# Reordering VectorE's weight splits among the turns of a dilated attention, with one early exponential on ScalarE

## The chip, the cores and the metric

The kernel runs on one core of a Trainium2 chip. The metric is the device time in microseconds (us) of one execution; lower is better. The engines of the core work in parallel, each through its own list of instructions in order, and meet only at semaphores: TensorE (PE, with its weight loads as PEld), VectorE (DVE), ScalarE (ACT), GpSimd (POOL) and SyncE (SP), which issues the transfers.

## The reference

Four layers of a transformer on 256 tokens of width 1024: two layers of a first kind (feed-forward, mixer, feed-forward), whose mixers differ, and two of a second kind. All is float32. The change lies in the mixer of the second layer, the "odd" one:

```python
def odd_mixer(h, w_in, w_out, q_g, k_g, pool_w, pool_scale):
    q, k, v, u = jnp.split(h @ w_in, [hd, 2 * hd, 3 * hd], axis=-1)
    q = rms_norm(q.reshape(b, s, DIL_HEADS, HEAD_DIM), q_g)      # 8 heads of 64
    k = rms_norm(k.reshape(b, s, DIL_HEADS, HEAD_DIM), k_g)
    outs, ms, ls = zip(*[dilated_branch(q, k, v, w, d) for w, d in DIL_PAIRS])
    ms = jnp.stack(ms)
    wts = jnp.stack(ls) * jnp.exp(ms - jnp.max(ms, axis=0))
    att = jnp.einsum('rbsh,rbshd->bshd', wts, jnp.stack(outs).astype(jnp.float32))
    att = (att / jnp.sum(wts, axis=0)[..., None]).astype(h.dtype)
    pool = multiscale_pool(u, pool_w, pool_scale)
    return jnp.concatenate([att.reshape(b, s, hd), pool], axis=-1) @ w_out
```

The three dilated branches are folded into one attention: scores plus a mask, an exponential, and a multiplication of the exponentials by a table that holds how many branches see each key. Then `x = x + mix`, and a feed-forward block on `rms_norm(x)` follows.

## The kernel before

**Weights.** All weights of the kernel go through one plan of units, mostly 128 x 1024 floats. SP brings unit u into one of six `staging` buffers; ACT makes its high part `whi` (line 1222); DVE subtracts to get the low part `wlo` (line 1710). Both parts live in rings of four buffers, so ACT may make `whi` of unit u only when PE has used unit u - 4. PE multiplies each pair of high and low parts three times (lines 591 to 593) in the mixers, or by the lines 640 and 642 in the feed-forward blocks. The pair "ACT split, DVE split" of one unit is called a split below. Each engine's program counts the splits that it owes in `side.due`, and `catch_up()` writes them out.

**The order.** Nothing is scheduled by a planner. Each engine's list is written by generators that `weave` runs in rounds: in each round every live generator writes its piece up to its next `yield`, and after the round, if a generator is still alive, `after` (here `catch_up`) writes the splits that are due.

**The odd stage, from 698 to 763 us of the trace.** The generator `dil` writes the attention, `pool` the pooled branch and then `down`, the multiplication by `w_out` (eight units, each in two halves of six matmuls). `attend` goes through eight groups of two heads (four for the first 128 tokens, four for the last 128) in turns. For a group i, in successive turns: PE makes the scores (line 833, "scores i"); DVE adds the mask and takes the maximum (line 1982, two instructions and 1991); ACT makes the exponential (line 1370); DVE multiplies by the table and sums (line 1968); PE transposes the result (line 820); ACT copies it out of PSUM (line 1361); PE multiplies it with v (line 807). After the fourth and the eighth group DVE takes the reciprocal of the sums (line 1945) and writes the attention's output of this half (line 1960, `od_o`). Groups are numbered 0 to 7.

**PSUM.** There are eight banks, handed out by the order of PE's program; who takes a bank waits until its last user's content was read. While `down` holds four of them, the scores of group i + 1 take the bank pair of the scores of group i, so PE's line 833 waits for DVE's line 1982 of the group before. The output of the second half (groups 4 to 7) takes the bank of the first half, so PE's line 807 of group 4 waits for DVE's line 1960 of the first half.

**The end of the stage.** DVE adds `down`'s result to x (line 1758, four instructions). `norm_T` then belongs to the next feed-forward block: PE transposes x in eight pieces (line 603), ACT writes the high part of each piece (`hT`, line 1235), DVE the low part (`hT`, line 1719), after which both write the splits still due. In the feed-forward block PE's first matmul (line 640) waits for the low parts of the pieces 0 and 1: its two banks held these pieces.

Of the kernel before, what the change touches and what calls it, by code (L numbers as in the profile page):

```python
# [10 lines left out]
ALU = mybir.AluOpType  # L11
ACT = mybir.ActivationFunctionType
# [176 lines left out]
def weave(gens, after=None):  # L189

    live, r = list(gens), 0
    while live:
        r += 1
        for item in list(live):
            if r >= item[0]:
                try:
                    next(item[1])
                except StopIteration:
                    live.remove(item)
        if live and after is not None:  # L200
            after()


def build(nc, A, out):
    ctx = ExitStack()
    with ctx:
        K = Count(nc, ctx)
# [1001 lines left out]
        def scalar_program(e):  # L1209
# [231 lines left out]
            def odd(m):  # L1441
                g = m.g
                norm_T(m)

                def project(q):
                    yield from x_cols(512)
                    by_token(g, 512 * q, 512, lambda t: m.qkv[:, t, q * 512:(q + 1) * 512])

                def norm(P, q):
                    sl = slice(512 * q, 512 * q + 512)  # L1450
                    head_norm(P, m.qkv[:, :, sl], m.hq[:, :, sl], [("in ev", g, 512 * q, t) for t in range(2)])

                weave([(1, project(1))], catch_up)
                norm("od k", 1)
                weave([(1, project(0))], catch_up)

                def pool():
                    for j0 in (0, 2):
                        yield
                        split()  # L1460
                        side.due += 1
                        yield
                    for k in range(3):
                        side.due += 1
                        yield
                    yield
                    by_token(g, 1024, 512, lambda t: m.qkv[:, t, 1024:1536])
                    side.due += 1

                def finish():  # L1470
                    for k in range(4):
                        e.wait_ge(*K.at("od pool mm", k))
                        e.activation(m.mh[:, 4 + k, :], bk("od pool", k)[:, 0:256], ACT.Copy,
                                     scale=m.psc[:, k:k + 1]).then_inc(*K.inc("pool_hi", ("od mh", k)))
                    yield
                    yield from down(m.rows)

                def dil():
                    norm("od q", 0)
                    yield  # L1480
                    e.wait_ge(*K.at("par", g))
                    heads_T("od k", 128, 4, m.kT, m.qg[:, 1:2])
                    heads_T("od q", 128, 4, m.qT, m.qg[:, 0:1])
                    yield
                    yield
                    turns = attend(m.at)
                    for _ in range(4):
                        next(turns)
                        yield
                    yield  # L1490
                    yield
                    yield from turns
                    transposed("dil", 4, m.mh[:, 0:4, :])

                weave([(1, dil()), (1, pool()), (9, finish())], catch_up)
# [203 lines left out]
        def vector_program(e):  # L1699
# [63 lines left out]
            def down(g, rows, coef):  # L1763
                for k in range(len(rows)):
                    for n in range(2):
                        if k + 1 == len(rows):
                            for t in range(2):
                                residual(g, coef, t, n)
                        if n and k + 2 < len(rows):
                            side.due += 1  # L1770
                        if n == 0 or k + 1 < len(rows):
                            yield
                side.due += 2
# [133 lines left out]
            def transposed(P, nk, dh, dl, *last):  # L1907
                for k0 in range(0, nk, 2):
                    e.wait_ge(*K.at(P + " oT hi", k0))
                    e.tensor_tensor(flat(dl[:, k0:k0 + 2, :]), bk(P + " oT", k0)[:, 0:512],  # L1910
                                    flat(dh[:, k0:k0 + 2, :]).bitcast(F32), ALU.subtract).then_inc(
                        *K.inc("oTl", (P + " oT", k0 // 2), ("ev", (P + " oT", k0)),
                               *(last if k0 + 2 == nk else ())))
# [9 lines left out]

                return e.tensor_tensor(x, x, r.unsqueeze(2).broadcast_to([128, H, 64]), ALU.mult)

            def attend(a):
                P, H = a.P, a.H
                groups = [(t, h0) for t in range(2) for h0 in range(0, H, 2)]
                mx = a.mx
                scale = a.scale if callable(a.scale) else lambda t, h: a.scale  # L1930
                for turn in range(H + 3):
                    if 0 <= turn - 2 < H and groups[turn - 2][1] == H - 2:

                        i = turn - 2
                        t, c0 = groups[i][0], groups[i][0] * 8
                        l, r = mx[:, 2, c0:c0 + H], mx[:, 3, c0:c0 + H]
                        if a.mult is None:
                            e.wait_ge(*K.at(P + " ex", i))
                        else:
                            e.wait_ge(*K.at(P + " pm", i))  # L1940
                        if a.sink is not None:
                            e.wait_ge(*K.at(P + " sink", t))
                            e.tensor_tensor(l, l, r, ALU.add).then_inc(*K.inc("att_sum"))
                            e.wait_ge(*K.now("att_sum"))
                        e.reciprocal(r, l).then_inc(*K.inc("att_sum", (P + " one by", t)))
                    if 0 <= turn - 3 < H:
                        t, h0 = groups[turn - 3]
                        if h0 == H - 2:
                            r = mx[:, 3, t * 8:t * 8 + H]
                            e.wait_ge(*K.at(P + " one by", t))  # L1950
                            e.wait_ge(*K.at(P + " pv", turn - 3))
                            if a.crossed:
                                o = a.dst[:, t, :].rearrange("p (j i e) -> p i j e", j=2, i=4)
                                src = bk(P + " o", t)[:, 0:512].rearrange("p (i j e) -> p i j e", i=4, j=2)
                                rr = r.rearrange("p (i j) -> p i j", i=4).unsqueeze(3).broadcast_to([128, 4, 2, 64])
                            else:
                                o = a.dst[:, t, :].rearrange("p (h e) -> p h e", h=H)
                                src = bk(P + " o", t)[:, 0:H * 64].rearrange("p (h e) -> p h e", h=H)
                                rr = r.unsqueeze(2).broadcast_to([128, H, 64])
                            e.tensor_tensor(o, src, rr, ALU.mult).then_inc(  # L1960
                                *K.inc("att_sum", (P + " o", t), ("ev", (P + " o", t))))
                    if 0 <= turn - 1 < H and a.mult is not None:
                        i = turn - 1
                        t, h0 = groups[i]
                        nk, c0 = 128 * (t + 1), t * 8 + h0
                        e.wait_ge(*K.at(P + " ex", i))
                        for j in range(2):
                            e.tensor_tensor_reduce(out=a.sm[i % 3][:, j, 0:nk], in0=a.sm[i % 3][:, j, 0:nk],
                                                   in1=a.mult(t), scale=1.0, scalar=0.0, op0=ALU.mult, op1=ALU.add,
                                                   accum_out=mx[:, 2, c0 + j:c0 + j + 1]).then_inc(  # L1970
                                *K.inc("att_pm", *([(P + " pm", i)] if j else [])))
                    if turn < H:
                        i = turn
                        t, h0 = groups[i]
# [141 lines left out]
            def odd(m):  # L2116
# [17 lines left out]
                def pool():  # L2134
# [44 lines left out]
                    side.due += 1  # L2179
                    yield  # L2180
                    yield from down(g, m.rows, 1.0)

                def dil():
                    head_norm("od q", m.hq[:, :, 0:512], m.hr[0][:, :, :], 8, 64, 64.0)
                    yield
                    yield
                    yield
                    e.wait_ge(*K.at("consts", 1))
                    e.wait_ge(*K.at("od q", "hn"))
                    turns = attend(m.at)  # L2190
                    for _ in range(4):
                        next(turns)
                        yield
                    yield
                    yield
                    yield from turns
                    transposed("dil", 4, m.mh[:, 0:4, :], m.ml[:, 0:4, :])

                weave([(1, dil()), (1, pool())], catch_up)

            def mixer2(m):
                g, P, N = m.g, m.P, m.N
# [506 lines left out]
```

## Time and profile before

| | |
|---|---|
| three runs | 1801.32, 1804.37, 1805.64 us; median 1804.37 |
| the profiled execution | 1804.61 us, of which the span of the trace 1802.8 |
| PE busy | 1778.0 us, 99% of the span |
| DVE busy | 1272.8 us, 71% |
| ACT busy | 947.8 us, 53% |
| 16 transfer engines, main queue | 56.4% of their time |
| granted TensorE clock, mean | 0.998 of full speed |

PE is busy all the time, and 90% of the chain of work that ended last lies on it. In the odd stage the chain leaves PE several times for ACT and DVE. A time in the rows is in us from the span's start.

### The profile page before, as it was taken

Reading aid. Unit: us, or ns where it says so; the run is one execution under the profiler, and the core shown is the slowest. Engines: PE = TensorE matmul, PEld = TensorE weight load, DVE = VectorE, ACT = ScalarE, POOL = GpSimd, SP = SyncE. Lnnn points to the kernel's source line nnn. Section 1 sums busy time; section 2 is a strip of 40 time slices with the busy share of each in tenths; the row PEclk is TensorE's granted clock in tenths of the full one; section 3 lists DMA queues with packets and bytes.
Section 4 is the critical chain, followed back from the end, with each engine's and each line's share of the span. In section 5 each row is a group of like instructions: output and inputs, shape, how many; then the busy total and the mean of one; then the engine's idle time right before and its main releaser. Section 6 shows DMA issues by size and latency. Waiting matters only on the chain.

```text
span 1802.8 us, 24902 instructions
## 1 busy us (share of the span) xinstructions
PE 1778.0 (99%) x9704; PEld 1512.2 (84%) x9704; DVE 1272.8 (71%) x1932; ACT 947.8 (53%) x1344; POOL 30.1 (2%) x38
## 2 busy tenths in 40 slices
PE   8999999999999999999999999999999999999998
PEld 7888888888888888788888788888888878888886
DVE  6775795776577657677656967777756778677774
ACT  5554655555455545565535545455544644555553
POOL 0000000000000001000000000000000000000000
PEclk9999999999999999999999999999999999999999
DMA  8666523666566655366666534556665443456663
GB/s 252 197 179 199 174 83 92 197 184 194 167 203 186 194 174 181 106 188 189 196 186 179 171 113 130 183 181 188 193 191 172 141 154 123 157 185 191 190 194 106
DMA packets 227614, 309.25 MB, mean 172 GB/s; under 512 B 22494, under 2 KB 176254, under 8 KB 227498
## 3 DMA queue, kind: packets, MB, share of 16 engines
q1 hardware_dynamic: 227334, 307.35, 56.4%
q8 instruction: 78, 1.28, 0.3%
q14 instruction: 38, 0.31, 0.1%
q10 hardware_dynamic: 164, 0.30, 0.1%
HBM read 306.57 MB, written 1.05 MB: 171 GB/s over the span
## 4 chain that ended last, share of the span: by engine, by line
PE 90%; DVE 6%; ACT 2%; issue 1%; DMA 1%; SPq 0%; DVEq 0%; POOLq 0%; POOL 0%; ACTq 0%
PE ps L640 26%; PE ps L591 15%; PE ps L593 15%; PE ps L592 15%; PE ps L642 13%; DVE wlo L1710 2%; PE ps L1132 1%; PE ps L603 1%; PE ps L807 1%; DVE ev_acc L1719 1%; PE ps L833 1%; ACT whi L1222 1%; PE ps L820 1%; PE ps L775 0%; DVE m_scr L1719 0%
## 5 line engine op out<-in xcount | busy, mean ns | idle before, releaser
L1710 DVE TENSOR_TENSOR wlo<-staging,whi 128x1024 fp32r<-128x1024 f32 (+1 forms) x582 | 695.0, 1211 | 344.9 <-ACT whi L1222 344.6
L1222 ACT ACTIVATE whi<-staging 128x1024 fp32r<-128x1024 f32 (+1 forms) x582 | 608.1, 1050 | 484.8 <-PE ps L593 297.9
L640 PE MATMUL ps<-hT,whi 128*128 128x512 f32 x1984 | 624.5, 396 | 0.0
L642 PEld LDWEIGHTS ps<-hT,wlo 128*128 128x128 f32 x1984 | 373.0, 188 | 88.2
L642 PE MATMUL ps<-hT,wlo 128*128 128x256 f32 x1984 | 390.0, 278 | 0.0
L640 PEld LDWEIGHTS ps<-hT,whi 128*128 128x128 f32 x1984 | 302.4, 189 | 0.2 <-DVE hT L1719 0.2
L591 PE MATMUL ps<-whi,fh 128*128 128x512 f32 (+1 forms) x528 | 206.0, 390 | 0.4 <-DVE wlo L1710 0.4
L592 PE MATMUL ps<-wlo,fh 128*128 128x512 f32 (+1 forms) x528 | 205.5, 389 | 0.0
L593 PE MATMUL ps<-whi,fl 128*128 128x512 f32 (+1 forms) x528 | 205.3, 389 | 0.0
L591 PE MATMUL ps<-whi,hT 128*128 128x512 f32 (+3 forms) x464 | 184.7, 398 | 0.8 <-DVE wlo L1710 0.6
L593 PE MATMUL ps<-whi,hT 128*128 128x512 f32 (+3 forms) x464 | 177.4, 382 | 0.0
L592 PE MATMUL ps<-wlo,hT 128*128 128x512 f32 (+3 forms) x464 | 177.0, 381 | 0.0
L591 PEld LDWEIGHTS ps<-whi,fh 128*128 128x128 f32 (+1 forms) x528 | 99.1, 188 | 22.6 <-DVE wlo L1710 2.3
L593 PEld LDWEIGHTS ps<-whi,fl 128*128 128x128 f32 (+1 forms) x528 | 99.1, 188 | 20.7
L592 PEld LDWEIGHTS ps<-wlo,fh 128*128 128x128 f32 (+1 forms) x528 | 99.1, 188 | 20.3
L591 PEld LDWEIGHTS ps<-whi,hT 128*128 128x128 f32 x464 | 87.2, 188 | 21.4 <-issue 3.8
L593 PEld LDWEIGHTS ps<-whi,hT 128*128 128x128 f32 x464 | 87.2, 188 | 16.2
L592 PEld LDWEIGHTS ps<-wlo,hT 128*128 128x128 f32 x464 | 87.4, 188 | 14.3 <-issue 0.5
L1293 ACT ACTIVATE fh<-sg 128x512 fp32r<-128x512 f32 x62 | 39.2, 632 | 114.0 <-DVE sg L1812 114.0
L1797 DVE TENSOR_TENSOR sg<-sg,R 128x512 f32<-128x512 f32 x124 | 85.8, 692 | 4.3
L1794 DVE TENSOR_TENSOR sg<-ps,sg 128x512 f32<-128x512 f32 x124 | 84.9, 684 | 0.2
L591 PE MATMUL ps<-hT,whi 128*128 128x256 f32 x288 | 82.8, 287 | 0.0
(328 smaller groups left out, 1870.2 us busy)
## 6 DMA issues: line engine op xcount, KB each, us to landing
staging<-in_w_in SPq DMA_DIRECT2D x92, 512.0 KB, 3.6
staging<-in_ffn_w_down SPq DMA_DIRECT2D x88, 512.0 KB, 4.2
staging<-in_ffn_w_gate SPq DMA_DIRECT2D x84, 512.0 KB, 4.3
staging<-in_ffn_w_up SPq DMA_DIRECT2D x84, 512.0 KB, 4.5
staging<-in_w_ffn_gate SPq DMA_DIRECT2D x44, 512.0 KB, 4.5
staging<-in_w_ffn_up SPq DMA_DIRECT2D x44, 512.0 KB, 4.5
staging<-in_w_ffn_down SPq DMA_DIRECT2D x44, 512.0 KB, 4.2
staging<-in_od_w_in SPq DMA_DIRECT2D x16, 512.0 KB, 4.4
```

The source lines that it names most:

```text
L591: e.matmul(o, lh, rh, start=start, stop=False)
L592: e.matmul(o, lh, rl, start=False, stop=False)
L593: return e.matmul(o, ll, rh, start=False, stop=stop)
L603: w = e.transpose(ps[:, t * 128:t * 128 + 128], xs[:, t, k * 128:k * 128 + 128], ident)
L640: e.matmul(o, wh[:, kk, j * 128:j * 128 + 128], hT[:, k, :], start=k == 0, stop=False)
L642: m = e.matmul(o[:, 0:256], wl[:, kk, j * 128:j * 128 + 128], hTh[:, k, :], start=False, stop=k == KD - 1)
L807: w = e.matmul(ops[t][:, (h0 + j) * 64:(h0 + j) * 64 + 64], a.pt[i % 2][:, o:o + 128], a.vN(kt, h0 + j), start=kt == 0, stop=kt == t)
L1222: e.activation(whi[u % NH][:, 0:n], stage[u % NS][:, 0:n], ACT.Copy).then_inc(*K.inc("hi", ("hi", u)))
L1293: e.activation(f.fh[:, 2 * p:2 * p + 2, :], s[:, :, 0:256], ACT.Copy).then_inc(*K.inc("fh", ("fh", g, p, 0)))
L1710: e.tensor_tensor(wlo[u % NH][:, 0:n], stage[u % NS][:, 0:n], whi[u % NH][:, 0:n].bitcast(F32), ALU.subtract).then_inc(*K.inc("lo", ("lo", ...
L1794: e.tensor_tensor(ss, PS[:, b:b + 2, 0:256], ss, ALU.add).then_inc(*K.inc("ps_r", *[("ev", u) for u in users]))
L1797: e.tensor_tensor(ss, ss, R22, ALU.mult).then_inc(*K.inc("ps_r", ("scaled", g, p, part)))
```

## The change

In the odd stage, three things. On DVE, `attend` gets a parameter `between`, and the multiplication by the table (line 1968 before) moves ahead of the block of line 1960; between the two `between()` writes the splits that are due. For the odd stage `between` is `catch_up`, and `dil` also calls `catch_up` in its rounds without a turn. `weave` gets no `after` any more there. At the end `dil` goes on until `pool` has finished (`over`), and a last `catch_up()` follows the `weave`. On ACT, one exponential of one column is written two rounds ahead of the turns, its result in a column that nothing reads. The other attentions have no table and no `between`; their order stays.

```diff
+                    e.activation(m.at.mx[:, 3, 8:9], m.qg[:, 0:1], ACT.Exp).then_inc(*K.inc("exp"))
                     yield
                     turns = attend(m.at)
...
-            def attend(a):
+            def attend(a, between=lambda: None):
...
+                    if 0 <= turn - 1 < H and a.mult is not None:
+                        ...
+                                *K.inc("att_pm", *([(P + " pm", i)] if j else [])))
+                    between()
                     if 0 <= turn - 3 < H:
...
                     yield from down(g, m.rows, 1.0)
+                    over.append(True)
+
+                over = []
...
                     yield
-                    yield
-                    yield
+                    for _ in range(2):
+                        catch_up()
+                        yield
...
-                    turns = attend(m.at)
+                    turns = attend(m.at, catch_up)
...
                     yield from turns
                     transposed("dil", 4, m.mh[:, 0:4, :], m.ml[:, 0:4, :])
-
-                weave([(1, dil()), (1, pool())], catch_up)
+                    while True:
+                        yield
+                        catch_up()
+                        if over:
+                            return
+
+
+                weave([(1, dil()), (1, pool())])
+                catch_up()
```

What this does to the lists of the engines, at three places. Names in the rows: `od_0` to `od_2` are the exponentials of three groups in turn, `od_3` and `od_4` their transposes, `od_5` maxima and sums. In the changed kernel the line numbers are higher: 1710 is 1712, 1968 is 1955, 1960 is 1974, 1982 is 1986, 1719 is 1721. An ISA row on two heads is the multiplication or the masked maximum of one head.

First place: DVE, from the scores of group 5 to the scores of group 6. Before:

```order
L1991 TENSOR_SCALAR od_5<-od_5 128x2 [waits s_att_mx]
L1710 TENSOR_TENSOR wlo0<-staging,whi0 128x1024 [waits s_hi]
L1960 TENSOR_TENSOR od_o<-ps,od_5 128x512 [waits s_att,s_att_sum]
L1968 ISA od_2,od_5<-od_2,cst 128x256 [waits s_exp]
L1968 ISA od_5 128x1
L1982 ISA od_0,od_5<-ps,cst,od_hr0 128x256 [waits s_att]
```

In the changed kernel:

```order
L1995 TENSOR_SCALAR od_5<-od_5 128x2 [waits s_att_mx]
L1955 ISA od_2,od_5<-od_2,cst 128x256 [waits s_exp]
L1955 ISA od_5 128x1
L1712 TENSOR_TENSOR wlo0<-staging,whi0 128x1024 [waits s_hi]
L1974 TENSOR_TENSOR od_o<-ps,od_5 128x512 [waits s_att,s_att_sum]
L1986 ISA od_0,od_5<-ps,cst,od_hr0 128x256 [waits s_att]
```

The split and the output of the first half stood ahead of the multiplication of group 5 and now stand behind it. (Each multiplication and each masked maximum has a second pair of rows for the second head.)

Second place: DVE, the end of the odd stage. Before:

```order
L1710 TENSOR_TENSOR wlo1<-staging,whi1 128x1024 [waits s_hi]
L1758 TENSOR_TENSOR xs<-ps,xs 128x512 [waits s_prod] x4
L1719 SCALAR_TENSOR_TENSOR hT<-ps,gcol,hT 128x256 [waits s_hTh] x8
L1710 TENSOR_TENSOR wlo2<-staging,whi2 128x1024 [waits s_hi]
L1710 TENSOR_TENSOR wlo3<-staging,whi3 128x1024 [waits s_hi]
```

In the changed kernel:

```order
L1712 TENSOR_TENSOR wlo1<-staging,whi1 128x1024 [waits s_hi]
L1760 TENSOR_TENSOR xs<-ps,xs 128x512 [waits s_prod] x4
L1712 TENSOR_TENSOR wlo2<-staging,whi2 128x1024 [waits s_hi]
L1712 TENSOR_TENSOR wlo3<-staging,whi3 128x1024 [waits s_hi]
L1721 SCALAR_TENSOR_TENSOR hT<-ps,gcol,hT 128x256 [waits s_hTh] x8
```

Two splits moved from behind the eight low parts to ahead of them. On ACT the same place is unchanged:

```order
L1222 ACTIVATE whi2<-staging 128x1024
L1235 ACTIVATE hT<-ps,gcol 128x256 x8
L1222 ACTIVATE whi3<-staging 128x1024
```

ACT writes `whi2` ahead of its eight high parts and `whi3` behind them, in both kernels.

Third place: ACT, ahead of the first turn. Before:

```order
L1337 ACTIVATE od_qT<-ps,od_qg 128x512 x2
L1222 ACTIVATE whi0<-staging 128x1024
L1222 ACTIVATE whi1<-staging 128x1024
L1222 ACTIVATE whi2<-staging 128x1024
L1222 ACTIVATE whi3<-staging 128x1024
L1370 ACT_TABLE_LOAD
L1370 ACTIVATE od_0<-od_0,od_5 128x128 x2
```

In the changed kernel:

```order
L1337 ACTIVATE od_qT<-ps,od_qg 128x512 x2
L1222 ACTIVATE whi0<-staging 128x1024
L1222 ACTIVATE whi1<-staging 128x1024
L1486 ACT_TABLE_LOAD
L1486 ACTIVATE od_5<-od_qg 128x1
L1222 ACTIVATE whi2<-staging 128x1024
L1222 ACTIVATE whi3<-staging 128x1024
L1370 ACTIVATE od_0<-od_0,od_5 128x128 x2
```

The load of the exponential's table moved ahead of two splits, with the one-column exponential behind it.

## Rows read from the trace of the kernel before

**Rows 1.** The page, part 1: busy us (share of the span), instructions.
```profile
PE 1778.0 (99%) x9704; PEld 1512.2 (84%) x9704; DVE 1272.8 (71%) x1932; ACT 947.8 (53%) x1344; POOL 30.1 (2%) x38
```

**Rows 2.** Waits, 700 to 765 us: us in total, times, longest us.
```profile
PE ps L820 <- DVE od L1968: 1.6, 3, 0.9
...
PE ps L787 <- DVE od_o L1960: 0.9, 1, 0.9
```

**Rows 3.** ACT in order of time: start us, us, instruction [idle before <- releaser].
```profile
707.67 1.06 ACT L1222 ACTIVATE whi<-staging 128x1024 fp32r<-128x1024 f32 x1 [3.85 <-PE ps L593]
709.11 1.06 ACT L1222 ACTIVATE whi<-staging 128x1024 fp32r<-128x1024 f32 x1 [0.37 <-PE ps L593]
710.19 1.28 ACT L1370 ACT_TABLE_LOAD   x1
711.48 0.70 ACT L1370 ACTIVATE od<-od 128x128 f32<-128x128 f32 x2
```

**Rows 4.** PE in order of time, three places of the turns.
```profile
723.91 1.89 PE L951 MATMUL ps<-od_pl,od_pw 128*128 128x256 f32 x8
...
729.90 0.70 PE L833 MATMUL ps<-od_kT,od_qT 64*128 64x256 f32 x4 [0.21 <-DVE od L1982]
...
735.26 1.10 PE L807 MATMUL ps<-od_qkv,od 128*128 128x64 f32 x8
```

**Rows 5.** DVE in order of time, end of the pooling and groups 3 and 4.
```profile
723.05 0.22 DVE L2170 TENSOR_TENSOR od_pl<-od_pl,od_u 128x64 f32<-128x64 f32 x1
...
727.30 1.23 DVE L1710 TENSOR_TENSOR wlo<-staging,whi 128x1024 fp32r<-128x1024 f32 x1 [0.43 <-ACT whi L1222]
728.44 0.28 DVE L1968 CUSTOM_DVE_ANT_0 od<-od,cst 128x128 f32<-128x128 f32 x1
...
728.86 0.48 DVE L1982 CUSTOM_DVE_ANT_0 od<-ps,cst,od_hr 128x256 f32<-128x256 f32 x1
```

**Rows 6.** ACT in order of time, the exponentials of groups 3 and 5.
```profile
727.43 0.69 ACT L1370 ACTIVATE od<-od 128x128 f32<-128x128 f32 x2
...
733.73 0.90 ACT L1370 ACTIVATE od<-od 128x256 f32<-128x256 f32 x2
```

**Rows 7.** DVE in order of time, groups 5 and 6.
```profile
734.52 0.68 DVE L1960 TENSOR_TENSOR od_o<-ps,od 128x512 f32<-128x512 f32 x1
735.12 0.42 DVE L1968 CUSTOM_DVE_ANT_0 od<-od,cst 128x256 f32<-128x256 f32 x1
...
735.81 0.48 DVE L1982 CUSTOM_DVE_ANT_0 od<-ps,cst,od_hr 128x256 f32<-128x256 f32 x1
```

**Rows 8.** DVE in order of time, the end of the stage.
```profile
759.34 2.74 DVE L1758 TENSOR_TENSOR xs<-ps,xs 128x512 f32<-128x512 f32 x4 [1.02 <-PE ps L593]
762.11 3.22 DVE L1719 SCALAR_TENSOR_TENSOR hT<-ps,gcol,hT 128x256 fp32r<-128x256 f32 x8
```

**Rows 9.** ACT in order of time, the same stretch.
```profile
758.71 1.06 ACT L1222 ACTIVATE whi<-staging 128x1024 fp32r<-128x1024 f32 x1 [1.66 <-PE ps L593]
761.60 3.03 ACT L1235 ACTIVATE hT<-ps,gcol 128x256 fp32r<-128x256 f32 x8 [1.82 <-PE ps L603]
764.47 1.11 ACT L1222 ACTIVATE whi<-staging 128x1024 fp32r<-128x1024 f32 x1
```

**Rows 10.** PE in order of time, the same stretch.
```profile
761.18 2.10 PE L603 MATMUL ps<-cst,xs 128*128 128x128 f32 x16
763.08 0.70 PE L640 MATMUL ps<-hT,whi 128*128 128x512 f32 x2
```

**Rows 11.** Stretches of the even stage: PE, PEld, DVE, ACT, POOL busy; PEclk, transfers.
```profile
277.80:281.07 3.27, 2.70 (x25) 2.73 (x26) 1.71 (x3) 2.93 (x4) 0.00 (x0) 1.00 0.00 0
281.07:284.48 3.41, 3.41 (x10) 2.64 (x10) 0.64 (x3) 0.35 (x1) 0.70 (x1) 0.50 0.00 0
```

**Rows 12.** PE in order of time, the same stage.
```profile
278.37 1.06 PE L787 MATMUL ps<-cst,ev_o 128*128 128x128 f32 x8 [1.17 <-DVE ev_o L1960]
...
279.27 1.84 PE L914 MATMUL ps<-cst,ev_sqc 128*128 128x1 f32 x16
```

More of the change, by code:

```diff
@@ L1945, in attend @@
                         e.reciprocal(r, l).then_inc(*K.inc("att_sum", (P + " one by", t)))
+                    if 0 <= turn - 1 < H and a.mult is not None:
+                        i = turn - 1
+                        t, h0 = groups[i]
+                        nk, c0 = 128 * (t + 1), t * 8 + h0
+                        e.wait_ge(*K.at(P + " ex", i))
+                        for j in range(2):
+                            e.tensor_tensor_reduce(out=a.sm[i % 3][:, j, 0:nk], in0=a.sm[i % 3][:, j, 0:nk],
+                                                   in1=a.mult(t), scale=1.0, scalar=0.0, op0=ALU.mult, op1=ALU.add,
+                                                   accum_out=mx[:, 2, c0 + j:c0 + j + 1]).then_inc(
+                                *K.inc("att_pm", *([(P + " pm", i)] if j else [])))
+                    between()
                     if 0 <= turn - 3 < H:
@@ L1961, in attend @@
                                 *K.inc("att_sum", (P + " o", t), ("ev", (P + " o", t))))
[L1962 to L1971, printed above, removed]
                     if turn < H:
@@ L2193, in dil @@
                         yield
-                    yield
-                    yield
+                    for _ in range(2):
+                        catch_up()
+                        yield
                     yield from turns
                     transposed("dil", 4, m.mh[:, 0:4, :], m.ml[:, 0:4, :])
-                weave([(1, dil()), (1, pool())], catch_up)
+                    while True:
+                        yield
+                        catch_up()
+                        if over:
+                            return
+                weave([(1, dil()), (1, pool())])
+                catch_up()
             def mixer2(m):
```

## The prediction

> **What bounds the kernel now.** I read the page's busy times first: PE is busy 99% of the span [rows 1]. Whatever holds PE up is paid in full, and what happens on DVE, ACT or the transfer queues counts only where PE waits for it. The waits of the odd stage come next: PE stands 1.6 us before its transposes (line 820) for DVE's multiplication by the table, and once 0.9 us (line 787) for the attention's output [rows 2]. That is about 2.5 us, and it is all that a better order of the turns can give back. Then I read the three engines side by side, in order of time, wherever the new lists differ: in the turns, and at the end of the stage. The end of the stage is the place that a reader of the diff misses.
>
> **The change part by part.**
>
> *The early exponential.* Before, ACT finishes a split at 710.17, loads the table for 1.28 us and starts the first exponential at 711.48 [rows 3]. Now the load lies ahead of the split that starts at 707.67, where ACT stood idle for 3.85 us waiting for PE [rows 3]. Load and one short exponential, under 2 us together, vanish in that idle stretch, so they cost nothing; were it absent they would cost 1.28 us and a bit. The first exponential starts 1.28 us earlier, the first multiplication follows, and the first transposes, one of the waits in [rows 2], are no longer late: some 0.6 us for PE.
>
> *The splits behind the multiplication, turns 1 to 3.* A split holds DVE 1.14 us from start to start (727.30 to 728.44) [rows 5]. Taken out from ahead of the second multiplication, it lets that one run 1.14 us earlier, and PE's longest wait of 0.9 us [rows 2] goes. PE is then about 1.3 us ahead. But it next needs the pooled tensor, which ends 723.05 + 0.22 = 723.27 on DVE, while PE starts on it at 723.91 [rows 5, 4]: a margin of 0.64. DVE has no idle time there to give up, since it does the same work in another order; I find it 0.1 us earlier at most. So PE is about 0.7 us ahead at the pooling matmuls.
>
> *Group 3 and 4.* Before, DVE waits for ACT's high part, does the split at 727.30, and meets the exponential of group 3 (ended 728.12) at 728.44; the scores of group 4 start at 728.86 [rows 5, 6]. Now the exponential ends at 728.12 - 0.67 = 727.45. Multiplication 0.42, then the split 1.14, then the scores: 729.05 in place of 728.86. The split, which filled DVE's wait for the exponential, now stands between the multiplication and the scores. PE's scores of group 5 wait for the scores of group 4 to be read, since they share the banks; they started at 729.90 [rows 4], now at about 730.1. The lead of 0.7 us is gone and PE is 0.2 us behind.
>
> *Group 5 and 6.* The same thing, larger. The exponential of group 5 runs 733.73 to 734.63 [rows 6]; 0.2 later it ends at 734.8. Before, DVE did a split and the half's output (line 1960, started 734.52, over at 735.20) during that exponential, multiplied at 735.12 and began the scores of group 6 at 735.81 [rows 7]. Now it idles until 734.8, multiplies for 0.69 (735.12 to 735.81), splits for 1.14 and only then writes the output: 736.64, over at 737.32. PE's line 807 of group 4 takes the bank of that output. It began at 735.26, right behind the output [rows 4, 7]; now it begins at about 737.4. Price: 2.1 us, less at most 0.1 of a wait that stood there anyway. This shift carries through groups 6 and 7, for each of the following steps hangs on the one before (scores, exponential, multiplication, transposes), and the last split before the second output waits for PE's own progress. **The turns together: 2.0 us lost.** The bounds: 2.5 us gained, if the waits of [rows 2] go and nothing takes their place; 4 us lost, if a second split is exposed besides.
>
> *The end of the stage.* Before, DVE starts the low parts of the transposed x at 762.11, right after x [rows 8], and PE's first matmul of the feed-forward block starts at 763.08, as soon as the pieces 0 and 1 are there (762.11 + 2 x 0.40 + 0.05 = 762.96; 3.22 us for eight) [rows 8, 10]. Now two splits come first. The first finds its high part (ACT, 758.71) ready and takes 762.11 to 763.25. The second needs the high part that ACT writes behind its own eight high parts: it starts at 764.47 and ends at 765.58 [rows 9]. So DVE waits until 765.61, splits until 766.75, and then starts the low parts: pieces 0 and 1 are there at 767.6, and PE starts at 767.7 in place of 763.08. **4.6 us lost**, in which PE has nothing at all to do, since its transposes end at about 763.2 [rows 10]. Behind it PE needs 0.7 us per piece and DVE delivers one each 0.4 [rows 8, 10], so nothing more is lost; and nothing comes back, since the two splits were never late (they are the third and fourth unit of the block, wanted 5 us after its start). Bounds: 4 us, if ACT's split follows a little faster, and 5, by the durations of [rows 8, 9].
>
> *TensorE's clock.* After such a pause the clock is likely to fall. In the even stage, after a stretch in which PE idled 1.17 us before line 787 and then did sixteen matmuls of one column [rows 12], the granted clock was 0.50, the level of 1.2 GHz, for 3.41 us (281.07 to 284.48), against 1.00 (2.4 GHz) before [rows 11]. At half speed 3.41 us do the work of 1.7. The new pause is 4.6 us with nothing in it, longer than the thin stretch above. Price: **1.7 us**, between 0 and 3.4 (two such stretches). By the Trainium skill ("TensorE: Matmul & The Clock Gate", sections "What's actually happening" and "HAM oscillation"), an idle PE falls back to half clock, and the first matmuls behind a wait run cold; the trace's 0.50 behind a thin stretch agrees, and by that page the sum would hold the 1.7 us, by the mean clock of 0.998 alone it would not.
>
> *Transfers.* Splits set free the staging buffers. Five are 0.1 to 2 us later, two are earlier; the ring is six units deep and no PE wait in the stage names a transfer [rows 2]. Nothing.
>
> **The sum.** The profiled execution took 1804.61 us with a span of 1802.8, and the median of three runs is 1804.37; the rest around the span stays. 1804.6 + 2.0 + 4.6 + 1.7 = 1812.9 us.
>
> **The rivals.** *The clock stays up.* For it: PE was fully busy until 763, and it dropped only once in the span. Against it: the pause is the longest in the trace after the start. Time: 1804.6 + 6.6 = 1811.2. *The turns gain.* If the output of the first half isn't what holds PE at 735.26, the turns save about 1 us: 1804.6 - 1.0 + 4.6 + 1.7 = 1809.9. For it: the waits of [rows 2] are real and the split leaves their path. Against it: the output ends at 735.20 and PE starts at 735.26 [rows 4, 7], and the bank is the same. *The clock falls in the turns too*, at the 2.1 us pause before line 807: another 1.7, so 1814.6. *The other side: the end of the stage costs nothing.* This would be so if PE's transposes and bank waits, and not DVE's low parts, set the start at 763.08, and if DVE's second split found its high part ready. It decides at ACT's split of 764.47: done by 763.2, the low parts would be late by two splits, 2.3 us; only with both splits already done would it be nothing. With the turns gaining all of 2.5 us the time is 1802.1. Against it: ACT's list puts that split behind eight instructions of 3.03 us [rows 9]. *Only the turns cost*, the end being hidden: 1806.6.
>
> **How the numbers follow.** About 0.3% (5.4 us) is what a measurement of this kernel can tell from no change. Forecast with the clock falling once 0.50 (1812.9); clock stays 0.17 (1811.2); turns gain 0.15 (1809.9); clock falls twice 0.08 (1814.6); other side 0.05 (1802.1); only the turns 0.05 (1806.6). The line for slower is 1809.8. The first two and the fourth lie beyond it; the third sits on it and is split; of the rest a little is lost to scatter: slower 0.80, same 0.18, faster 0.02. The range leaves out the last two and the tails: 1808.0 to 1815.5.
>
> **What the new profile would show.** ACT's table load near 704 us, in idle time. PE's transposes of the first two groups without a wait. A wait of PE at line 807 of about 2 us for the output (line 1974), near 735 us. A wait of PE of about 4.5 us, or a gap of that length, between line 603 and line 640 at 765 us, with DVE's two splits ahead of its eight low parts and the second one waiting for ACT. A stretch with PEclk 0.50 behind it. The feed-forward blocks and the layers of the second kind of the same length as before. I am wrong if the stretch from line 603 to the first line 640 keeps its 1.9 us, or if the stage up to line 603 is shorter than before.

## The result, and the profile after

| | before | changed |
|---|---|---|
| median | 1804.37 us (1801.32 to 1805.92, 5 runs) | 1816.3 us (1811.78 to 1817.62, 5 runs) |
| ratio, changed to before | | 1.0059, 95% interval 1.0045 to 1.0073 |
| profiled execution | 1804.61 us, span 1802.8 | 1817.15 us, span 1815.4 |
| granted TensorE clock, mean | 0.998 | 0.994 |

The changed kernel is slower by 0.6%, which the ratio makes 10.6 us (8.1 to 13.2). The page's busy times of the changed kernel answer to [rows 1]:

```profile
PE 1783.8 (98%) x9704; PEld 1516.4 (84%) x9704; DVE 1273.0 (70%) x1932; ACT 948.3 (52%) x1345; POOL 30.1 (2%) x38
```

DVE and ACT do the same work in the same busy time. PE's busy time grew by 5.8 us though its instructions are the same, and the span by 12.6: PE worked slower for part of the time, and stood still for the rest. Where it stood still is in the waits of the changed kernel from 698 to 790 us (us in total, times, longest us), which answer to [rows 2]:

```profile
PE ps L640 <- DVE hT L1721: 4.4, 1, 4.4
...
PE ps L807 <- DVE od_o L1974: 2.0, 1, 2.0
...
PE ps L833 <- DVE od L1986: 1.1, 1, 1.1
...
PE ps L787 <- DVE od_o L1974: 0.9, 1, 0.9
```

PE's waits at line 820, at which the change was aimed, fell from 1.6 us to 0.3, and the 0.9 us at line 787 is as before. New are the waits at the lines 640, 807 and 833. In order of time on PE; the whole program of this trace runs 1.20 us behind the trace of before when the turns begin (line 775 at 699.09 against 697.89), so 1.20 is to be taken off to compare with [rows 4]:

```profile
717.35 0.41 PE L820 MATMUL ps<-cst,od 128*128 128x128 f32 x2 [0.18 <-DVE od L1955]
724.23 1.99 PE L951 MATMUL ps<-od_pl,od_pw 128*128 128x256 f32 x8 [0.35 <-DVE od_pl L2174]
731.17 0.70 PE L833 MATMUL ps<-od_kT,od_qT 64*128 64x256 f32 x4 [1.05 <-DVE od L1986]
738.50 1.10 PE L807 MATMUL ps<-od_qkv,od 128*128 128x64 f32 x8 [1.98 <-DVE od_o L1974]
```

The pooling matmuls start at 723.03 on the time axis of before, 0.88 us ahead of 723.91; the scores of group 5 at 729.97, level with 729.90; line 807 of group 4 at 737.30, 2.04 us behind 735.26. DVE's side of the last one, which answers to [rows 7]: it idles for the exponential, multiplies, splits, and writes the output last.

```profile
735.93 0.43 DVE L1955 CUSTOM_DVE_ANT_0 od<-od,cst 128x256 f32<-128x256 f32 x1 [1.93 <-ACT od L1370]
...
736.63 1.22 DVE L1712 TENSOR_TENSOR wlo<-staging,whi 128x1024 fp32r<-128x1024 f32 x1
737.76 0.68 DVE L1974 TENSOR_TENSOR od_o<-ps,od 128x512 f32<-128x512 f32 x1
```

The end of the stage, DVE, then ACT, then PE, for [rows 8 to 10]:

```profile
762.49 2.74 DVE L1760 TENSOR_TENSOR xs<-ps,xs 128x512 f32<-128x512 f32 x4 [1.02 <-PE ps L593]
765.14 1.22 DVE L1712 TENSOR_TENSOR wlo<-staging,whi 128x1024 fp32r<-128x1024 f32 x1
768.76 1.23 DVE L1712 TENSOR_TENSOR wlo<-staging,whi 128x1024 fp32r<-128x1024 f32 x1 [2.40 <-ACT whi L1222]
769.90 3.22 DVE L1721 SCALAR_TENSOR_TENSOR hT<-ps,gcol,hT 128x256 fp32r<-128x256 f32 x8
```

```profile
764.75 3.03 ACT L1235 ACTIVATE hT<-ps,gcol 128x256 fp32r<-128x256 f32 x8 [1.82 <-PE ps L603]
767.62 1.11 ACT L1222 ACTIVATE whi<-staging 128x1024 fp32r<-128x1024 f32 x1
```

```profile
764.33 2.10 PE L603 MATMUL ps<-cst,xs 128*128 128x128 f32 x16
770.87 0.81 PE L640 MATMUL ps<-hT,whi 128*128 128x512 f32 x2 [4.44 <-DVE hT L1721]
771.91 1.05 PE L640 MATMUL ps<-hT,whi 128*128 128x512 f32 x2
```

From line 603 to line 640 PE takes 6.54 us, where it took 1.90. The last row shows more: two matmuls of 512 columns span 1.05 us, against 0.70 in [rows 10]. The clock fell. Stretches of the changed kernel (PE, PEld, DVE, ACT, POOL busy; PEclk, transfers):

```profile
270.00:300.00 30.00, 27.87 (x137) 23.39 (x136) 14.04 (x26) 14.90 (x26) 0.70 (x1) 0.89 0.13 36
698.00:748.00 50.00, 46.28 (x290) 38.23 (x288) 34.57 (x108) 28.06 (x48) 2.90 (x1) 1.00 0.37 111
764.00:790.00 26.00, 21.56 (x121) 18.58 (x120) 15.24 (x25) 14.31 (x23) 0.70 (x1) 0.93 0.36 98
1000.00:1200.00 200.00, 197.88 (x1078) 161.93 (x1078) 152.04 (x296) 98.49 (x158) 3.40 (x3) 0.99 0.48 148
1400.00:1600.00 200.00, 197.63 (x1094) 163.03 (x1094) 149.49 (x305) 99.71 (x159) 3.40 (x3) 0.99 0.48 147
```

PEclk is below 1.00 after the pause, but also in the even stage (0.89; the same stretch of before has 0.94) and in the mixers of the two layers of the second kind (0.99 over 200 us is one stretch at 1.2 GHz, 3.4 us long), where no instruction was changed. What PE did ahead of the first of these two stretches, which begins at 1051.20:

```profile
1048.85 1.50 PE L1132 MATMUL ps<-m_scr 32*128 32x128 f32 x16 [0.88 <-DVE m_scr L1986]
```

**Three lengths** make all that follows comparable, since they do not hold what happened elsewhere in the execution. *Turns*: from the start of the first transposes of keys and queries (line 775) to the start of the transposes of x (line 603). *Pause*: from there to the first line 640; 2.1 us of it are the transposes, so PE's own wait is shorter (4.44 us of the 6.54). *Block*: from there to the transposes at the end of the feed-forward block (line 603, 943.89 before, 953.22 after). Before they are 63.29, 1.90 and 180.81 us; in the changed kernel 65.24, 6.54 and 182.35. The differences are 1.95, 4.64 and 1.54, together 8.13 us. The other 4.5 us of the difference of the spans lie outside: 1.2 ahead of line 775, and 3.2 in the two mixers, 1.6 for each stretch at 1.2 GHz. The experiments ask what causes the 8.1, and whether the 4.5 belong to the change. The profiled execution, at 1817.15 us, is one of the slower ones of the five.

### The profile page after: what moved, and what is told of

It reads as the page before. It is cut to its first block, busy times and chain, and to the rows that moved or that the text cites. A ratio compares the mean times of both kernels' runs of the same rounds, so it can differ in the third digit from the quotient of the medians.

```text
span 1815.4 us, 24903 instructions
## 1 busy us (share of the span) xinstructions
PE 1783.8 (98%) x9704; PEld 1516.4 (84%) x9704; DVE 1273.0 (70%) x1932; ACT 948.3 (52%) x1345; POOL 30.1 (2%) x38
## 3 DMA queue, kind: packets, MB, share of 16 engines
HBM read 306.57 MB, written 1.05 MB: 169 GB/s over the span
## 4 chain that ended last, share of the span: by engine, by line
PE 89%; DVE 6%; ACT 2%; issue 1%; DMA 1%; SPq 0%; DVEq 0%; POOLq 0%; POOL 0%; ACTq 0%
PE ps L640 26%; PE ps L591 15%; PE ps L592 14%; PE ps L593 14%; PE ps L642 13%; DVE wlo L1712 2%; PE ps L1132 1%; PE ps L807 1%; PE ps L603 1%; DVE ev_acc L1721 1%; ACT whi L1222 1%; PE ps L833 1%; PE ps L820 1%; PE ps L775 0%; DVE m_scr L1721 0%
```

## The experiments

All times are medians of each kernel's runs and of the kernel before on the same chip; the ratio is of the two, with its 95% interval. The lengths are those of one trace each.

**The end of the stage alone.** In the kernel before:

```diff
                 weave([(1, dil()), (1, pool())], catch_up)
+                catch_up()
```

> The kernel before, with one line more on VectorE: the two splits that are due at the end of the odd stage are written ahead of the low parts of the transposed x, as in the changed kernel. Theory (the end of the stage costs 4.6 us, the clock 1.7): the turns keep their length (63.3 us from line 775 to line 603), the stretch from the transposes (line 603) to the first matmul of the feed-forward block (line 640) grows from 1.9 to 6.5 us, a stretch of 1.2 GHz follows, and the time is about 6.3 us above before. Rival (the delay at the end is a follow-up of the slower turns): the stretch stays near 1.9 us and the time near before.

1811.13 us against 1804.66, ratio 1.0035 (1.0023 to 1.0048). Turns 63.30, pause 6.54, block 183.09. On PE:

```profile
763.97 2.10 PE L603 MATMUL ps<-cst,xs 128*128 128x128 f32 x16
770.51 1.19 PE L640 MATMUL ps<-hT,whi 128*128 128x512 f32 x2 [4.44 <-DVE hT L1719]
```

One line at the end makes the whole pause, to the hundredth of a microsecond, with unchanged turns. The clock fell already within the pause and stayed down behind it (PEclk by stretch):

```profile
768.20:770.50 2.30, 0.00 (x0) 0.02 (x1) 2.10 (x4) 2.21 (x5) 0.00 (x0) 0.61 0.42 147
770.50:775.10 4.60, 4.59 (x14) 3.93 (x15) 2.34 (x7) 0.14 (x2) 0.70 (x1) 0.50 0.41 118
```

So this block lost 2.3 us to the clock, not 1.5. 4.64 + 2.28 = 6.9 us for this trace; the ratio of the medians makes 6.3 (4.2 to 8.7 by the interval). The theory holds, the rival is out.

**The turns alone.** In the changed kernel, the last `catch_up()` taken out, and the end of `dil` turned round so that nothing is written once `pool` has finished:

```diff
                     while True:
                         yield
-                        catch_up()
                         if over:
                             return
+                        catch_up()
...
                 weave([(1, dil()), (1, pool())])
-                catch_up()
```

> The changed kernel with the end of the stage as before: the two splits behind the low parts again. Theory: the stretch from line 603 to line 640 is back at 1.9 us, the turns stay 2.0 us longer (65.2 us from line 775 to line 603), and the time is about 2 us above before. Rival (the clock alone makes the excess over the pauses, also in other stages): the time stays more than 4 us above before.

1808.45 us against 1804.66, ratio 1.0019 (1.0008 to 1.0029), that is 3.4 us (1.4 to 5.2). Pause 1.90, block 180.80: the end is repaired. Whether the time is about 2 us above before or over 4, the interval does not say; the lengths decide. The turns took 66.79 us, not 65.2. The clock tells why:

```profile
734.00:737.40 3.40, 2.43 (x14) 2.10 (x16) 1.89 (x7) 0.37 (x1) 0.00 (x0) 0.77 0.54 149
737.40:741.00 3.60, 3.60 (x19) 2.59 (x18) 1.76 (x9) 1.65 (x4) 0.00 (x0) 0.74 0.01 5
```

Behind the wait of 2 us at line 807 the clock was down, which it was not in the changed kernel's first trace. That asked for more traces, below.

**The early exponential alone.** In the kernel before:

```diff
                     heads_T("od q", 128, 4, m.qT, m.qg[:, 0:1])
                     yield
+                    e.activation(m.at.mx[:, 3, 8:9], m.qg[:, 0:1], ACT.Exp).then_inc(*K.inc("exp"))
                     yield
```

> The kernel before, with the early exponential alone. Theory: the table load goes into ScalarE's idle stretch, the first transposes come 0.6 us earlier, but the second ones wait for VectorE, which has no idle time there, so the stage keeps its length within 0.2 us (63.3 us from line 775 to line 603) and the time is that of before. Rival (the load was on the path): the stage is 0.6 to 1.3 us shorter.

1803.64 us against 1804.66, ratio 0.999 (0.9979 to 1.0002). Turns 62.73, that is 0.56 us shorter: the theory missed, and the rival's lower end is right. The load is in idle time, as expected:

```profile
704.94 1.28 ACT L1485 ACT_TABLE_LOAD   x1
706.23 0.20 ACT L1485 ACTIVATE od<-od_qg 128x1 f32<-128x1 f32 x1
708.77 1.06 ACT L1222 ACTIVATE whi<-staging 128x1024 fp32r<-128x1024 f32 x1 [2.34 <-PE ps L593]
```

What I had overlooked is one idle time of DVE in the kernel before, ahead of the first multiplication:

```profile
710.51 1.21 DVE L1710 TENSOR_TENSOR wlo<-staging,whi 128x1024 fp32r<-128x1024 f32 x1
712.21 0.29 DVE L1968 CUSTOM_DVE_ANT_0 od<-od,cst 128x128 f32<-128x128 f32 x1 [0.48 <-ACT od L1370]
```

From start to start a split takes 1.14 us, so the multiplication could have begun at 711.65, 0.56 us earlier. Here the multiplication follows the split at once, and all that DVE does up to the pooled tensor, a stretch in which it has no other idle time, comes 0.56 earlier.

**Behind the multiplication in the first turns only.** Written as a change of the kernel of the turns alone: the early exponential; `between()` behind the multiplication, which is back behind the output; and from the fifth turn on the splits at the head of the turn as before; the end as before:

```diff
                 for turn in range(H + 3):
+                    if turn > 3:
+                        between()
...
-                    if 0 <= turn - 1 < H and a.mult is not None:
-                        i = turn - 1
...
-                    between()
                     if 0 <= turn - 3 < H:
                         t, h0 = groups[turn - 3]
...
+                    if 0 <= turn - 1 < H and a.mult is not None:
+                        i = turn - 1
...
+                    between()
                     if turn < H:
```

> The early exponential, and the splits behind the multiplication in the turns of the groups 0 to 2 only; from the fourth group on, and at the end of the stage, the order of before. Theory (a split is free where other work already fills VectorE's wait for the exponential, and costs where it was that filling): PE reaches the pooling matmuls 0.7 us earlier and keeps it, so the stage is 0.7 us shorter (62.6 us). Rival (the new place costs in every turn): the stage is as long as before or longer.

1803.81 us against 1804.66, ratio 0.9993 (0.9981 to 1.0005). Turns 62.54, 0.75 shorter, as forecast. With the run before it: 0.56 of that is the early exponential, 0.19 the splits. PE's long wait before the second transposes is gone, and the pooled tensor takes its place as the bound:

```profile
714.23 0.41 PE L820 MATMUL ps<-cst,od 128*128 128x128 f32 x2 [0.18 <-DVE od L1973]
721.11 1.99 PE L951 MATMUL ps<-od_pl,od_pw 128*128 128x256 f32 x8 [0.35 <-DVE od_pl L2176]
727.20 0.70 PE L833 MATMUL ps<-od_kT,od_qT 64*128 64x256 f32 x4 [0.19 <-DVE od L1988]
```

The scores of group 5 wait 0.19 us here and 1.05 in the changed kernel; that is the exposed split of group 3.

**One split ahead of the low parts, not two.** In the kernel before:

```diff
                 weave([(1, dil()), (1, pool())], catch_up)
+                side.due -= 1
+                split()
```

> The kernel before, with only the first of the two due splits ahead of the low parts of the transposed x; its high part is ready. Theory (each step on VectorE's list ahead of the low parts counts with its own length, and the wait for ScalarE comes on top with the second split only): line 603 to line 640 takes 1.9 + 1.1 = 3.0 us, the clock stays up behind so short a pause, the time is about 1.1 us above before. Rival (any wait at this place loses the clock): a stretch of 1.2 GHz follows and the time is 2.8 us above.

1806.83 us against 1804.25, ratio 1.0011 (0.9999 to 1.0023). Pause 2.92, block 180.80: 1.02 us more and no loss of clock behind it. PE's own wait was 0.81 us:

```profile
764.49 0.70 PE L640 MATMUL ps<-hT,whi 128*128 128x512 f32 x2 [0.81 <-DVE hT L1719]
```

**Both splits ahead, and ScalarE's high part ahead too.** The end of the first experiment, with the same line in ACT's program:

```diff
                 weave([(1, dil()), (1, pool()), (9, finish())], catch_up)
+                catch_up()
```

> Both splits ahead of the low parts on VectorE, and on ScalarE the high part of the second one ahead of its eight high parts of x; all else as before. Theory (half of the 4.6 us is VectorE waiting for a high part that ScalarE writes behind eight others): VectorE splits without a wait, 2 x 1.14 us, and line 603 to line 640 takes 1.9 + 2.3 = 4.2 us instead of 6.5. Rival (the pause is set by ScalarE's high parts or by TensorE's banks): it stays near 6.5 us.

1808.65 us against 1804.25, ratio 1.0022 (1.001 to 1.0033). Pause 4.04, block 182.36. DVE's two splits run without a gap, and PE itself waits 1.94 us:

```profile
761.30 2.35 DVE L1711 TENSOR_TENSOR wlo<-staging,whi 128x1024 fp32r<-128x1024 f32 x2
763.57 3.22 DVE L1720 SCALAR_TENSOR_TENSOR hT<-ps,gcol,hT 128x256 fp32r<-128x256 f32 x8
```

```profile
764.53 1.11 PE L640 MATMUL ps<-hT,whi 128*128 128x512 f32 x2 [1.94 <-DVE hT L1720]
```

Two splits cost 2.1 us, and the other 2.5 of the 4.64 were DVE's wait for the one high part. The clock fell here as well, behind a wait of 1.94 us, and cost 1.56 us of the block.

**The output ahead of the split.** The kernel of the turns alone, with the order multiplication, output, split:

```diff
                     if 0 <= turn - 1 < H and a.mult is not None:
...
-                    between()
                     if 0 <= turn - 3 < H:
                         t, h0 = groups[turn - 3]
...
+                    between()
                     if turn < H:
```

> The changed kernel's turns (multiplication first), but with the output of a half (od_o) ahead of the split instead of behind it; the end of the stage as before. Theory (TensorE's line 807 of group 4 waits for the output's bank, and so for what stands ahead of the output): its wait of 2.0 us shrinks by a split, to 0.9 us, of which line 833 takes some back; at the end of the turns line 787 no longer waits its 0.9 us; the stage is 63.5 us long from line 775 to line 603, against 65.2. Rival (line 807 waits for something else): the wait stays at 2.0 us.

1804.92 us against 1804.25, ratio 1.0001 (0.9991 to 1.0012). On PE:

```profile
732.64 1.10 PE L807 MATMUL ps<-od_qkv,od 128*128 128x64 f32 x8 [0.85 <-DVE od_o L1973]
734.67 0.95 PE L833 MATMUL ps<-od_kT,od_qT 64*128 64x256 f32 x4 [0.48 <-DVE od L1986]
```

The wait at line 807 lost one split (1.98 to 0.85), line 833 took 0.48 back, and line 787 waits no more. The turns were 65.10 us, though, not 63.5, and the clock was down between 735 and 739 us (PEclk 0.57). So the theory of the wait holds and its rival is out; the length of the stage was missed, which asked for a second trace as well.

**Both gains together.** The kernel of the first turns only, where the last turn (the one with the second output) also writes its split behind the output:

```diff
-                    if turn > 3:
+                    if 3 < turn < H + 2:
```

> The early exponential, splits behind the multiplication in the first turns only, and in the last turn the second half's output ahead of the split; the end of the stage as before. Theory: the 0.7 us of the first turns and the 0.9 to 1.0 us that line 787 waited add up, since both lie on TensorE's path: stage 61.5 us against 63.3, time 1.8 us (0.1%) below before, hardly more than the runs can resolve. Rival (one wait only takes the other's place): stage 62.5 us.

1802.97 us against 1804.25, ratio 0.999 (0.9979 to 1.0001). Turns 61.42, 1.87 shorter. All that PE still waits from 690 to 760 us:

```profile
PE ps L951 <- DVE od_pl L2176: 0.4, 1, 0.4
PE ps L820 <- DVE od L1973: 0.3, 2, 0.2
PE ps L833 <- DVE od L1988: 0.2, 1, 0.2
```

The two gains add up, as both lie on PE's path. The trace shows the 1.9 us plainly; the runs do not separate them from nothing, since the interval just includes 1. The medians differ by 1.3 us.

**Second traces.** Four kernels once more, unchanged: the kernel before, the changed kernel, the turns alone, and the output ahead of the split.

> The kernel before once more, for a second trace. Theory (stretches of 1.2 GHz in the mixers of the second half come and go from run to run, whatever the odd stage does): the odd stage is 63.3 us from line 775 to line 603 and 1.9 us to line 640 again, while the number of stretches at 1.2 GHz elsewhere may differ from the first trace, with some 1.6 us for each. Rival (they belong to the changed kernel): this trace has none in the mixers of the second half, like the first one.

> The changed kernel once more. Theory (the pause of 4.4 us at line 640 itself brings the clock down): a stretch of 1.2 GHz begins within the pause or right behind it again; the stage is 65.2 us and the pause the same to 0.1 us. Rival (the drop was chance): no stretch of 1.2 GHz there.

> The changed turns with the end of before once more. Its first trace had a stretch of 1.2 GHz within the turns and a stage of 66.8 us, the changed kernel had none there and 65.2 us. Theory (a pause of 2 us brings the clock down in some runs only): 65.2 us without such a stretch, 66.8 with one, nothing between but parts of a stretch. Rival (the end of the stage acts back on the turns): 66.8 us again without a stretch.

> The output ahead of the split, once more. Its first trace had the expected waits (line 807 0.85 us, line 787 none), and a stage of 65.1 us in place of 63.5, with a stretch of 1.2 GHz in the turns. Theory: where no such stretch falls in the turns the stage is 63.5 us. Rival (something else in this order costs 1.6 us): 65.1 us without a stretch.

Single times: 1803.29, 1814.73, 1810.62 and 1803.94 us, with 1804.07 for the kernel before beside them. With the lengths of all traces, and whether PEclk was below 1.00:

| trace | turns | clock down in the turns | pause | block |
|---|---|---|---|---|
| before | 63.29 | no | 1.90 | 180.81 |
| before, again | 63.25 | no | 1.91 | 180.79 |
| early exponential | 62.73 | no | 1.91 | 180.79 |
| first turns only | 62.54 | no | 1.90 | 180.80 |
| both gains | 61.42 | no | 1.90 | 180.80 |
| one split ahead | 63.31 | no | 2.92 | 180.80 |
| both splits, ScalarE too | 63.33 | no | 4.04 | 182.36 |
| end alone | 63.30 | no | 6.54 | 183.09 |
| turns alone | 66.79 | yes | 1.90 | 180.80 |
| turns alone, again | 66.80 | yes | 1.90 | 180.81 |
| output first | 65.10 | yes | 1.90 | 180.80 |
| output first, again | 63.58 | no | 1.90 | 180.80 |
| changed | 65.24 | no | 6.54 | 182.35 |
| changed, again | 66.79 | yes | 6.53 | 183.19 |

The changed kernel's second trace has what the first had not, the low clock in the turns, and a longer one behind the pause:

```profile
698.00:748.00 50.00, 46.25 (x276) 37.64 (x275) 33.49 (x106) 26.75 (x47) 2.90 (x1) 0.97 0.33 105
764.00:790.00 26.00, 21.57 (x116) 18.52 (x115) 14.45 (x23) 14.23 (x22) 0.70 (x1) 0.87 0.32 90
1000.00:1200.00 200.00, 197.83 (x1087) 162.25 (x1087) 152.73 (x296) 100.02 (x158) 3.40 (x3) 1.00 0.46 148
1400.00:1600.00 200.00, 197.65 (x1102) 163.14 (x1101) 150.29 (x307) 100.61 (x159) 3.40 (x3) 1.00 0.46 148
```

And it has no stretch at 1.2 GHz in the mixers (1.00 from 1000 to 1200 and from 1400 to 1600 us), where the first trace had two. So the same kernel has the 3.2 us in the mixers or not. The turns alone are such a pair too: two in the first trace, none in the second. The second trace of the kernel before has none, like its first, which fits either side of that expectation. Traces of kernels that are not slower have them: the second one of the output-first kernel has both, at 1803.94 us. Of the 14 traces nine have one or two of them, and nothing ties their number to the odd stage. The even stage, unchanged in all 14, is as fickle: the low clock shows there in ten, for 3.4 us or for 6.8.

For the turns: of six traces with the order of the changed kernel or its variant with the output first, four had the low clock there, at about 1.55 us each (65.24 and 66.79; 63.58 and 65.10); of eight traces with the other orders none had. With the changed kernel's own order it is three of four. So the turns alone are 66.8 us only with such a stretch, as that theory had it; the output-first kernel is 63.6 us without one, as forecast; and the changed kernel's second trace has the forecast drop behind the pause, but turns of 66.79 us in place of the 65.2 that I expected.

For the pause: each of four traces with a pause of 4 us or more (PE's own wait 1.94 us in one, 4.44 in three) lost 1.5 to 2.4 us of clock in the block, none of the ten others did.

## Why the prediction was right, and where it was off

The direction and the mechanism were right; the size was low. 1812.9 us was forecast and 1816.3 measured as a median, 0.8 above the upper end of 1815.5. The ratio, 1.0059, makes 1815.0 us of the median of before, inside the range, with 1812.5 to 1817.5 as its interval. Point by point:

*The end of the stage, 4.6 us.* Measured 4.64, alone as in the whole. Both steps were tried: the splits' own time (1.0 for one, 2.1 for two), and the wait for ScalarE by taking it away (2.5 less). "The other side", that the end costs nothing, is out.

*The turns, 2.0 us.* Measured 1.95 where the clock stayed up. The steps on the way are as told: PE level again with the scores of group 5 (forecast 730.1, measured 729.97 on the time axis of before), line 807 at 737.3 (forecast 737.4), held by the bank of the output, which the output-first kernel shows by shortening exactly this wait by one split. One sum on the way is slightly off: 727.45 + 0.42 + 1.14 makes 729.01 for the scores of group 4, not 729.05; measured 728.94. "The turns gain" is out.

*The early exponential.* I let it be worth 0.6 us for the first transposes and nothing beyond, with the words that DVE "has no idle time there to give up" and would be "0.1 us earlier at most". That step failed: the idle time was the one that the load itself had made. With the early exponential alone its removal moved all of DVE's work up to the pooled tensor by 0.56. In the changed kernel the first multiplication, now ahead of its split, still waits 0.19 us for the exponential, and the pooled tensor is 0.29 us earlier (ended 722.98 on the time axis of before, against 723.27). In the sum this changed little, since the exposed split of group 3 took it back; it is why PE was 0.88 ahead at the pooling matmuls, not 0.7.

*The clock behind the pause, 1.7 us.* Measured 1.54 and 2.4 in the two traces of the changed kernel (block 182.35 and 183.19 against 180.80), and 2.3 with the end alone. It came each time. The cases with it held 0.73 of the chance; "the clock stays up" is out here, and is what the pause of one split (2.92 us, PE's own wait 0.81) showed. The words that the clock "dropped only once in the span" of before are a misreading: it also dropped at 1800.00 us, in the last 2.8 us of the span. And the clock fell behind a wait of 1.94 us as well, in the experiment with ScalarE's part ahead too, so the wait did not have to be as long as the 4.6 us with which I argued.

*The clock in the turns.* This is the term that the sum put at nothing. It was the rival with the chance 0.08 ("the clock falls in the turns too", 1814.6 us). It fell in four of the six traces of such turns. The sum with it is 8.1 + 1.55 = 9.7 us, or 10.5 with the longer low stretch behind the pause, against 10.6 by the ratio. The rows for a better chance were there: in the even stage 1.17 us of idle time next to thin matmuls had been enough [rows 11, 12], and the 2.1 us that I had worked out for line 807 stand among thin matmuls too. I used these rows for the price only. That the stage of the first trace came out at 8.1 us more, so near to the forecast 8.3, was luck: it is the one of the four traces with this order in which the clock stayed up in the turns.

*Outside the stage.* Nothing was forecast, and nothing is owed to the change as far as the traces go. Both low stretches in the mixers of the first trace stand behind a wait of 0.88 us and sixteen small matmuls; the kernel before has the same two waits, 0.88 us each, and no fall in either trace. Why one execution falls and another does not was not found. It goes with the scatter between runs of one and the same kernel: of 35 runs of the kernel before, the seven with a mean granted clock of 0.999 took 1801.4 to 1802.5 us, the nine with 0.995 or 0.996 took 1806.7 to 1809.8.

## What to carry to other kernels

A piece of work that fills an engine's wait costs nothing where it stands, and can cost its full length in a place where another engine waits behind it: before moving it "off the critical path", look at what its engine will do in its old place, and at what waits behind its new one. After rewriting loops that share a counter of work owed, compare the last lines written as well as the ones meant: here one `catch_up()` behind the loop cost 6.3 us, more than the turns it was written for. Where PE is the bound, a new wait of some 2 us may have to be paid twice, once for its length and once, at half clock, for the matmuls behind it: 1.94 and 4.44 us behind the transposes did so in all four traces, 2.0 us in the turns in three of four.

## What the runs showed of the hardware

The granted clock fell in four of six traces in which PE waited in the turns (2.0 us at line 807 in one order, three times in four; 0.85 and 0.48 close together in the other, once in two; in both orders about 1.0 us more, at line 833, 6 to 7 us earlier), at about 1.55 us each. That it takes so short a wait, and comes and goes with the same program, was unexpected: the same list of instructions took 65.24 or 66.79 us here, and nothing between. By the Trainium skill ("TensorE: Matmul & The Clock Gate", section "HAM oscillation") TensorE's waits of about 3 to 5 us between bursts of matmuls bring it back to half clock. The traces agree behind the waits of 4.44 us, and show the same behind waits of 1.9 to 2.0 us, which that section does not have. The price in this kernel was 1.5 to 2.4 us each.
